# Attention stage of a two-layer decoder trunk: the same work per block in another order on each engine, norms cut in two, two buffers for queries and keys

## Chip, cores and metric

The kernel runs on all 8 cores of one Trainium2 chip, each core with its own share of the batch and no exchange between cores. The metric is the device time of the slowest core, in microseconds (us). In one execution of the kernel before, the median time was 3305.33 us over 3 runs (3304.32 to 3310.04).

## What is computed

One inference step of a two-layer decoder trunk. Layer 0 is a convolution module and a dense gated feed-forward network; from its output, keys and values are projected once. Layer 1 is what this document is about: sliding-window attention (16 query heads and 4 key heads of 64 channels, window 128, a learned sink per head, RMS-norm of every query and key head), then a top-2-of-8 expert network. Of the reference, cut to the part around attention:

```python
s = rms_norm(h, norm_kv); k = rms_norm((s @ w_k).reshape(..., 4, 64), k_norm); v = s @ w_v
q = rms_norm((rms_norm(h, norm_mix[1]) @ w_q).reshape(..., 4, 4, 64), q_norm)
s = einsum(q, k) * 64 ** -0.5            # query block n reads key blocks n-1 and n
e = exp(where(mask, s, -inf) - m); den = sum(e) + exp(sink - m)
h = h + (e / den @ v) @ w_o
hn = rms_norm(h, norm_ffn[1])            # goes to the router and to the experts
top_vals, top_idx = top_k(hn @ w_router + b_router, 2)
```

## The kernel before

A core has a prompt of 2048 rows, cut into 16 blocks of 128, and 16 sample rows as a seventeenth block (number 16, which goes first). The stages follow each other: convolution, dense feed-forward, its down projection with the gated embedding, attention with routing, experts, final stage. The attention stage is the loop at the end of `build`, 21 iterations i = 0 to 20, written out by hand as a software pipeline. Each engine executes its own instructions strictly in the order in which this loop issues them; semaphores are set by the scheduler class from what each instruction reads and writes.

In iteration i, block ord5[i] is projected, the block before it has its queries and keys turned, the block two before it has its scores, softmax and product with the values, the block three before it has its output projection, and its norm for the experts and its routing follow. The parts, in the order of iteration i before:

1. `x3_norm` (L1563): SyncE loads the residual rows of a block two iterations ahead, into one of 6 buffers.
2. `x3_turn` (L1579): TensorE turns the normed block (8 transposes into one PSUM bank), ScalarE copies it out (L939).
3. `x3_scale` (L1569) of the next block: ScalarE squares and sums (L944), VectorE adds epsilon (L948), GpSimd raises to the power -1/2 (L949), ScalarE scales (L1576).
4. `x_turn` (L1776): the normed output block of two iterations before is turned and copied, for the router.
5. `scores` (L1681) for group 0: TensorE, 4 matmuls into PSUM banks 0 and 1 (L1693); ScalarE takes the exponential (L1699); VectorE multiplies by the mask (L1701).
6. `kv_mm` (L1588): 8 matmuls of 512 columns (L1595); ScalarE copies keys into `qkf` and values into a bf16 buffer.
7. scores for group 1; `o_turn` (L1737): the attention output is turned, VectorE copies it (L941).
8. `q_mm` (L1608) half 0 (L1614, 8 matmuls), copied by ScalarE into `qkf`.
9. `pv` (L1704) group 0 (L1720, 8 matmuls into banks 4 to 6), scores group 2, `route_l` (L343).
10. `q_mm` half 1, `qk_norm` (L1619): ScalarE squares 1280 columns (L1623), VectorE sums over each head (L1624, L1625), GpSimd raises 20 columns to the power -1/2 (L1626).
11. pv 1, scores 3, `oproj` (L1744) half 0 (L1751, 8 matmuls; VectorE adds the result to the residual rows, L1756), pv 2, a waiting `wave_b`.
12. `qk_turn` (L1662) of the block before, oproj half 1, `o_norm` (L1760): SyncE stores the residual rows; ScalarE squares, VectorE adds epsilon, GpSimd takes the power, VectorE scales with the gain (L1770).
13. pv 3, `onorm` (L1724): VectorE, 3 sums, a reciprocal and 3 products (L1728, L1729, L1732), which release banks 4 to 6.
14. `qk_scale` (L1629): VectorE scales keys (L1633) and queries (L1654) by the power, GpSimd multiplies the keys by the gain, twice (L1656).

All transposes and projections share three PSUM banks in rotation (`mb`, L1558), so that a group of matmuls waits until the result three groups before it has been copied out. The scores always use banks 0 and 1, so a group of scores waits for the exponential of the group before. `qkf` is one buffer.

Iterations 2 to 6 have the work of the sample rows at their end (`s_scores`, `s_scores2`, `s_values`, and `s_load` of the next cached keys and values), iteration 6 also the output projection, norm and routing of block 16 in one sequence. When 5, 5, 4, 2 blocks (and block 16 alone) are routed, `wave_a` (L360) issues a part of their slot arithmetic, and `wave_b` (L382) an iteration later the rest: small VectorE operations to L424, then two indirect DMAs per block, issued by GpSimd (L161), which scatter the normed rows to the experts' areas, then further VectorE operations from L432 on, which wait until the scatters have read the slot numbers. After the loop the last wave goes out, the expert weights are requested, and the rows of expert 0 are loaded.

Of the kernel before, what the change touches and what calls it, by code (L numbers as in the profile page):

```python
# [24 lines left out]
EPS = 1e-6  # L25
# [813 lines left out]
def build():  # L839
# [647 lines left out]
    curW = Cursor(O_S5W, Arena.SIZE)  # L1487
    curL = Cursor(11264, O_S5W)
# [16 lines left out]
    qkf, qkf_r = t5([128, 1280], F32, 0)  # L1505
# [63 lines left out]
    def x3_scale(n_):  # L1569
# [5 lines left out]
        powh(ms, rs, ms_r, rs_r, n)  # L1575
# [12 lines left out]
    def kv_mm(n_, n, xT, xT_r):  # L1588

        b = mb()  # L1590

# [14 lines left out]
        return vb, vb_r  # L1606

    def q_mm(n_, n, xT, xT_r, h):  # L1608
# [10 lines left out]
    def qk_norm(n_, n, vb, vb_r):  # L1619
# [7 lines left out]
        return n_, n, vb, vb_r, rs, r_  # L1627

    def qk_scale(n_, n, vb, vb_r, rs, r_):  # L1629
# [130 lines left out]
    def o_norm(n_):  # L1760
# [8 lines left out]
        powh(ms, rs, ms_r, rs_r, n)  # L1769
# [98 lines left out]
    for k in range(2):  # L1868
        x3_norm(ord5[k])
    s_load(0)  # L1870
    xs_ = x3_scale(ord5[0])
    waves = {}
    qn = qt = on = xn_ = lt = wv = None
    pend_wave = None
    done_l = []
    for i in range(17 + 4):
        a = ord5[i] if i < 17 else None
        s_ = ord5[i - 2] if 3 <= i < 19 else None
        if i + 2 < 17:
            x3_norm(ord5[i + 2])  # L1880
        xt = x3_turn(*xs_) if xs_ is not None else None
        xs_ = x3_scale(ord5[i + 1]) if i + 1 < 17 else None
        lt = x_turn(*xn_) if xn_ is not None else None
        xn_ = None
        if s_ is not None:
            scores(s_, 0)
        if xt is not None:
            vb = kv_mm(*xt)
        if s_ is not None:
            scores(s_, 1)  # L1890
        ot = None
        if on is not None:
            ot = o_turn(*on)
            on = None
        if xt is not None:
            q_mm(*xt, 0)
# [3 lines left out]
        if lt is not None:  # L1900
            b = mb()
            tl.route_l(*lt, b, 0)
            done_l.append(lt[0])
            lt = None
        if xt is not None:
            q_mm(*xt, 1)
            qn = qk_norm(xt[0], xt[1], *vb)
        if s_ is not None:
            pv(s_, 1)
            scores(s_, 3)  # L1910
        if ot is not None:
            oproj(*ot, 0)
        if s_ is not None:
            pv(s_, 2)
        if pend_wave is not None:
# [136 lines left out]
```

How the kernel before makes its waits and increments, by code:

```python
    def wait(self, e, key, val):  # L87
        if val <= self.waited[e].get(key, 0):
            return
        self.E[e].wait_ge(self.semh[key], val)
        self.waited[e][key] = val
# [38 lines left out]
    def op(self, e, fn, r=(), w=(), part=False):  # L130
        xr = [x for x in r if x.excl]
        if xr:
            r = [x for x in r if not x.excl]
            w = list(w) + xr
        self.deps(e, r, w, part)
        inst = fn(self.E[e])
        self.cnt[e] += 1
        inst.then_inc(self.semh[e], 1)
        self.mark((e, self.cnt[e]), r, w, part)
# [1 line left out]
    def _land(self, inst, sem, r, w, part):  # L141
        self.cnt[sem] += 16
        inst.then_inc(self.semh[sem], 16)
        self.mark((sem, self.cnt[sem]), r, w, part)
```

## Time and profile before

| | us |
|---|---|
| median of 3 runs | 3305.33 |
| the profiled execution, its own time | 3307.96 |
| its span, slowest core (core 6) | 3306.6 |
| spans of all cores | 3280.7 to 3306.6 |
| attention loop, first key/query power to first expert matmul (L549) | 1255.3 to 1817.8 |

The profiled execution is 2.6 us over the median, and its time is 1.4 us over its span. Over the span TensorE is busy 75%, VectorE 31%, ScalarE 23%, GpSimd 18% of the time. In the page, PE is TensorE's matmuls, PEld its weight loads, DVE is VectorE, ACT ScalarE, POOL GpSimd, SP SyncE. A group of instructions is named by line and operation; "idle before" is the time for which its engine stood still just before it, with what ended that wait. On the page the experts' matmuls (L549 and L577) make up 36% of the chain that ended last, and "issue", time in which the chain's engine waited for nothing that the profile shows, 11%.

### The profile page before, as it was taken

Reading aid. Unit: us, or ns where it says so; the run is one execution under the profiler, and the core shown is the slowest. Engines: PE = TensorE matmul, PEld = TensorE weight load, DVE = VectorE, ACT = ScalarE, POOL = GpSimd, SP = SyncE. Lnnn points to the kernel's source line nnn. Section 1 sums busy time; section 2 is a strip of 40 time slices with the busy share of each in tenths; the row PEclk is TensorE's granted clock in tenths of the full one; section 3 lists DMA queues with packets and bytes.
Section 4 is the critical chain, followed back from the end, with each engine's and each line's share of the span. In section 5 each row is a group of like instructions: output and inputs, shape, how many; then the busy total and the mean of one; then the engine's idle time right before and its main releaser. Section 6 shows DMA issues by size and latency. Waiting matters only on the chain.

```text
span 3306.6 us, 43794 instructions; the slowest of 8 cores (3280.7 to 3306.6 us)
## 1 busy us (share of the span) xinstructions
PE 2479.0 (75%) x18881; PEld 1703.1 (52%) x18967; DVE 1032.2 (31%) x1532; ACT 745.1 (23%) x1074; POOL 583.1 (18%) x760
## 2 busy tenths in 40 slices
PE   5395323899989926654652999999999999997344
PEld 2253111455534413332321889988789888886111
DVE  3175455222223313444452212121112212121454
ACT  4111232111112124443430112111112111110111
POOL 1001221000000003323223111111112111110444
PEclk8597667899999966887775999999999999999677
DMA  7734311633032251101015999999889999981553
GB/s 178 130 78 101 96 64 58 170 58 71 1 89 72 78 155 52 52 33 64 32 55 119 177 166 187 180 173 188 135 146 175 184 165 185 146 143 46 131 132 100
DMA packets 156202, 377.38 MB, mean 114 GB/s; under 512 B 52296, under 2 KB 61512, under 8 KB 155008
## 3 DMA queue, kind: packets, MB, share of 16 engines
q0 software_dynamic: 69360, 230.65, 41.2%
q1 hardware_dynamic: 81360, 133.08, 13.6%
q10 hardware_dynamic: 5280, 10.75, 1.0%
q8 instruction: 151, 2.47, 0.3%
q14 instruction: 51, 0.42, 0.0%
HBM read 510.48 MB, written 74.24 MB: 177 GB/s over the span
## 4 chain that ended last, share of the span: by engine, by line
PE 60%; issue 11%; DVE 9%; POOL 8%; DMA 6%; ACT 5%; ACTq 1%; SPq 1%; DVEq 0%; POOLq 0%
PE pb L549 24%; PE pb L577 12%; PE pb L1361 9%; PE pb L1416 4%; PE pb L1087 3%; DMA arena<-sc 2%; DVE arena L941 2%; POOL arena L1626 1%; POOL arena L822 1%; PE pb L1614 1%; POOL arena L949 1%; PE pb L1289 1%; ACT arena L944 1%; ACT arena L1268 1%; POOL arena L161 1%
## 5 line engine op out<-in xcount | busy, mean ns | idle before, releaser
L549 PE MATMUL pb<-arena 128*128 128x0 bf16 x7168 | 795.6, 274 | 0.8 <-DVE arena L510 0.8
L549 PEld LDWEIGHTS pb<-arena 128*128 128x128 bf16 x7168 | 675.6, 98 | 117.6 <-issue 1.1
L577 PE MATMUL pb<-arena 128*128 128x0 bf16 x3584 | 404.9, 274 | 0.0
L557 DVE TENSOR_TENSOR arena<-arena,pb 128x640 bf16<-128x640 f32 x224 | 184.0, 822 | 654.3 <-PE pb L549 654.3
L577 PEld LDWEIGHTS pb<-arena 128*128 128x128 bf16 x3584 | 336.0, 98 | 56.5
L1361 PE MATMUL pb<-arena 128*128 128x413 bf16 (+1 forms) x1760 | 312.0, 341 | 11.8 <-ACT arena L1367 7.7
L556 ACT ACTIVATE arena<-pb 128x640 f32<-128x640 f32 x224 | 157.5, 703 | 622.2 <-PE pb L549 622.2
L930 PE MATMUL pb<-arena 128*128 128x128 bf16 (+1 forms) x1180 | 103.6, 244 | 255.8 <-DVE arena L1770 112.7
L1361 PEld LDWEIGHTS pb<-arena 128*128 128x128 bf16 x1760 | 172.8, 98 | 150.6 <-ACT arena L1367 8.1
L930 PEld LDWEIGHTS pb<-arena 128*128 128x128 bf16 (+1 forms) x1180 | 80.7, 111 | 285.6 <-DVE arena L1770 115.6
L149 POOL DMA_DIRECT2D arena<-moe_gu x224 | 118.3, 545 | 590.2 <-PE pb L549 254.2
L1289 PE MATMUL pb<-arena 128*128 128x512 bf16 (+1 forms) x264 | 77.6, 460 | 165.6 <-ACT arena L1268 165.6
L805 PE MATMUL pb<-arena 128*128 128x512 bf16 (+1 forms) x269 | 91.7, 513 | 135.2 <-DMA arena<-arena 134.6
L944 ACT ACTIVATE arena<-arena 128x1024 bf16<-128x1024 f32 (+1 forms) x85 | 89.8, 1056 | 421.0 <-DVE arena L1421 179.6
L1416 PE MATMUL pb<-arena 128*128 128x512 bf16 (+1 forms) x732 | 164.4, 381 | 1.9 <-DVE arena L1368 0.7
L949 POOL TENSOR_TENSOR arena<-arena 128x1 f32<-128x1 f32 (+1 forms) x102 | 56.0, 549 | 527.7 <-DVE arena L948 527.6
L1368 DVE TENSOR_TENSOR arena<-arena,pb 128x413 bf16<-128x413 f32 (+1 forms) x110 | 64.2, 585 | 256.2 <-PE pb L1361 235.2
L939 ACT COPY arena<-pb 128x1024 bf16<-128x1024 bf16 (+6 forms) x142 | 112.4, 793 | 114.0 <-PE pb L1614 47.2
L1289 PEld LDWEIGHTS pb<-arena 128*128 128x128 bf16 (+1 forms) x272 | 30.2, 115 | 207.0 <-ACT arena L1268 163.9
L149 POOL DMA_DIRECT2D arena<-moe_d x128 | 67.5, 528 | 386.7 <-PE pb L549 379.3
L805 PEld LDWEIGHTS pb<-arena 128*128 128x128 bf16 (+1 forms) x272 | 32.6, 125 | 194.6 <-DMA arena<-arena 142.9
L1087 PE MATMUL pb<-arena 128*128 128x413 bf16 (+1 forms) x640 | 126.9, 364 | 4.9 <-ACT arena L939 4.9
(198 smaller groups left out, 2433.2 us busy)
## 6 DMA issues: line engine op xcount, KB each, us to landing
arena<-moe_gu POOLq DMA_DIRECT2D x224, 512.0 KB, 32.6
arena<-moe_d POOLq DMA_DIRECT2D x128, 448.0 KB, 33.7
arena<-x SPq DMA_DIRECT2D x32, 512.0 KB, 5.4
arena<-ffn_gu POOLq DMA_DIRECT2D x22, 512.0 KB, 5.7
XG<-arena ACTq DMA_DIRECT2D x1, 10240.0 KB, 33.4
arena<-XG SPq DMA_DIRECT2D x8, 1280.0 KB, 40.3
YD<-arena SPq DMA_DIRECT2D x8, 1280.0 KB, 22.4
h1D<-arena SPq DMA_DIRECT2D x16, 512.0 KB, 3.0
```

The source lines that it names most:

```text
L149: inst = self.E[q].dma_start(out=out, in_=in_)
L549: last = e.matmul(bank(b + h, HALF).shape_from_register(sr), w[:, a, kc, :], xg[:, kc, h * HALF:(h + 1) * HALF].shape_from_register(sr), s ...
L556: S.op("act", lambda e: e.activation(out=sg, in_=self.two(bG), func=AF.Silu), r=[b_r[bG], b_r[bG + 1]], w=[sg_r])
L557: S.op("dve", lambda e: e.tensor_tensor(out=self.hx[:, f, :].rearrange("p (h c) -> p h c", h=2), in0=sg, in1=self.two(bU), op=ALU.mult), r ...
L577: last = e.matmul(bank(b + h, HALF).shape_from_register(sr), w[:, k, :], self.hx[:, f, h * HALF:(h + 1) * HALF].shape_from_register(sr), s ...
L805: last = e.matmul(bank(bG + h2, 512, n), xT[:, kc, 0:n], self.Wg[kc // 2][:, kc % 2, h2 * 512:(h2 + 1) * 512], start=(kc == 0), stop=(kc = ...
L930: last = e.transpose(out=bankb(bk)[:, k * 128:k * 128 + n], in_=src[0:n, (k0 + k) * 128:(k0 + k + 1) * 128], identity=identb[0:n, 0:n])
L944: S.op("act", lambda e: e.activation(out=junk, in_=src, func=AF.Square, scale=1.0 / 32.0, accum_out=ms), r=r, w=[w, jr])
L1087: last = e.matmul(bank(bk_, n), W[:, a, kc, :], xnT[:, kc, s0:s0 + n], start=(kc == 0), stop=(kc == 7))
L1289: last = e.matmul(bank(bk + h, 512, n), zT[:, kc, i * 128:i * 128 + n], W2[:, kc, h * 512:(h + 1) * 512], start=(kc == 0), stop=(kc == 7))
L1361: last = e.matmul(bank(bk_, n), W[:, a, kc, :], xnT2[:, kc, s0:s0 + n], start=(kc == 0), stop=(kc == 7))
L1416: last = e.matmul(bank(bk + h_, 512, n), lt, Wd[:, f, h_ * 512:(h_ + 1) * 512], start=(f == 0), stop=(f == NF - 1))
```

## The change

Nothing of the matrix work is removed or added. `x3_scale` and `o_norm` are each cut into a part that squares (`x3_sq`, `o_sq`) and a part that scales (`x3_scale`, `o_scale`); in both, the addition of epsilon moves from VectorE to GpSimd. `qk_scale` moves from the end of the iteration to near the beginning of the next; its two GpSimd products become a part of their own, `kk_gain`. `qkf` has two buffers. Block 16's norm and routing ride along in iteration 7. The load of residual rows goes to the end of the iteration. The stage's weights lie 4096 bytes higher, so that the second buffer has room.

```diff
-    curW = Cursor(O_S5W, Arena.SIZE)
-    curL = Cursor(11264, O_S5W)
+    curW = Cursor(O_S5W + 4096, Arena.SIZE)
+    curL = Cursor(11264, O_S5W + 4096)
...
-    qkf, qkf_r = t5([128, 1280], F32, 0)
+    qkb = t5([128, 1280], F32, 2)
...
+    def powp(ms, rs, ms_r, rs_r, n):
+        S.op("pool", lambda e: e.tensor_scalar(out=ms, in0=ms, scalar1=EPS, scalar2=None, op0=ALU.add), w=[ms_r])
+        S.op("pool", lambda e: e.tensor_tensor(out=rs, in0=ms, in1=nhalf[0:n, 0:1], op=ALU.pow), r=[ms_r, c_eps], w=[rs_r])
+
+    def x3_sq(n_):
...
         square(h[0:n, :], xh[0:n, :], ms, n, [h_r], ms_r, xh_r)
-        powh(ms, rs, ms_r, rs_r, n)
+        powp(ms, rs, ms_r, rs_r, n)
+        return n_, n, h, h_r, rs, rs_r, xh, xh_r
+
+    def x3_scale(n_, n, h, h_r, rs, rs_r, xh, xh_r):
         S.op("act", lambda e: e.activation(out=xh[0:n, :], in_=h[0:n, :], func=AF.Copy, scale=rs), r=[h_r, rs_r], w=[xh_r])
...
+        return n_, qh, qh_r, kk, kk_r, vb, vb_r, k4, qkf_r
+
+    def kk_gain(n_, qh, qh_r, kk, kk_r, vb, vb_r, k4, qkf_r):
+        if n_ < 16:
             for u_ in range(2):
                 S.op("pool", lambda e: e.tensor_tensor(out=kk[:, :, u_, :], in0=k4, in1=gqk.unsqueeze(1).to_broadcast([128, 4, 64]), op=ALU.mult),
```

The loop body after, in the order of issue (`s_` is the block whose attention is made):

```python
if s_ is not None: scores(s_, 0)
xt = x3_turn(*xs_)                       # turn of block ord5[i]
qt = qk_scale(*qn)                       # of the block before
scores(s_, 1)
rs_ = [o_sq(n_) for n_ in (rn, r16) if n_ is not None]
kk_gain(*qt)
vb = kv_mm(*xt)
rs_ = [o_scale(*v) for v in rs_]
pv(s_, 0); scores(s_, 2)
ot = o_turn(*on)
xq = x3_sq(ord5[i + 1])
q_mm(*xt, 0, *vb[2:4])
pv(s_, 1); scores(s_, 3)
lts = [x_turn(*v) for v in rs_]
xs_ = x3_scale(*xq)
q_mm(*xt, 1, *vb[2:4]); qn = qk_norm(xt[0], xt[1], *vb)
qk_turn(*qt[0:7])
pv(s_, 2); oproj(*ot, 0)
pv(s_, 3); on = onorm(s_)
oproj(*ot, 1); rn = ot[0]
tl.wave_b(...)                           # if one is waiting
for lt in lts: tl.route_l(*lt, mb(), 0)
...                                      # sample work, wave_a
x3_norm(ord5[i + 2])
```

## Rows read from the trace of the kernel before

**Rows 1.** Stretches: us, busy us (and instructions) by engine, granted TensorE clock, DMA share, GB/s

```profile
950.00:1158.00 208.00, 200.71 (x1008) 93.63 (x1030) 72.89 (x82) 44.19 (x56) 15.17 (x27) 1.00 0.23 74
1579.00:1606.00 27.00, 17.95 (x130) 9.00 (x132) 12.08 (x27) 12.97 (x18) 7.38 (x5) 0.75 0.11 40
```

**Rows 2.** Timeline of GpSimd: power of 20 columns, once per block (start, us, what)

```profile
1255.26 3.53 POOL L1626 TENSOR_TENSOR arena<-arena 16x20 f32<-16x20 f32 x1 [8.70 <-DVE arena L1625]
...
1383.31 3.91 POOL L1626 TENSOR_TENSOR arena<-arena 128x20 f32<-128x20 f32 x1 [13.09 <-DVE arena L1625]
...
1551.96 3.91 POOL L1626 TENSOR_TENSOR arena<-arena 128x20 f32<-128x20 f32 x1 [13.62 <-DVE arena L1625]
...
1578.93 3.91 POOL L1626 TENSOR_TENSOR arena<-arena 128x20 f32<-128x20 f32 x1 [13.95 <-DVE arena L1625]
...
1606.06 3.91 POOL L1626 TENSOR_TENSOR arena<-arena 128x20 f32<-128x20 f32 x1 [14.12 <-DVE arena L1625]
...
1661.34 3.91 POOL L1626 TENSOR_TENSOR arena<-arena 128x20 f32<-128x20 f32 x1 [12.07 <-DVE arena L1625]
...
1701.07 3.91 POOL L1626 TENSOR_TENSOR arena<-arena 128x20 f32<-128x20 f32 x1 [9.28 <-DVE arena L1625]
```

**Rows 3.** Groups by line and shape, 1552 to 1660 us: count, busy us, mean ns, idle before

```profile
L1699 ACT ACTIVATE arena<-pb 128x1024 bf16<-128x1024 f32 x16 | 16.3, 1020 | 0.1
L939 ACT COPY arena<-pb 128x1024 bf16<-128x1024 bf16 x12 | 12.0, 999 | 1.2 <-PE pb L930 1.2
L1701 DVE TENSOR_TENSOR arena<-arena 128x1024 bf16<-128x1024 bf16 x16 | 11.0, 690 | 33.8 <-ACT arena L1699 33.8
L1656 POOL TENSOR_TENSOR arena<-arena 128x256 bf16<-128x256 f32 x8 | 9.9, 1242 | 16.6 <-DVE arena L1633 16.3
L1624 DVE TENSOR_REDUCE arena<-arena 128x20 f32<-128x1280 f32 x4 | 5.9, 1486 | 6.6 <-ACT arena L1623 6.6
L1756 DVE TENSOR_TENSOR arena<-pb,arena 128x512 f32<-128x512 f32 x8 | 5.5, 688 | 6.9 <-PE pb L1751 6.9
L1770 DVE SCALAR_TENSOR_TENSOR arena<-arena 128x1024 bf16<-128x1024 f32 x4 | 5.1, 1284 | 2.9 <-POOL arena L949 2.9
L1623 ACT ACTIVATE arena<-arena 128x1280 f32<-128x1280 f32 x4 | 5.1, 1270 | 0.1
L1654 DVE TENSOR_TENSOR arena<-arena 128x1024 bf16<-128x1024 f32 x4 | 4.9, 1224 | 0.1
L949 POOL TENSOR_TENSOR arena<-arena 128x1 f32<-128x1 f32 x8 | 4.4, 547 | 8.6 <-DVE arena L948 8.6
```

**Rows 4.** Timeline inside one plain iteration

```profile
1586.24 1.03 PE L930 MATMUL pb<-arena 128*128 128x128 bf16 x8 [3.55 <-DVE arena L1770]
...
1591.97 1.15 ACT L1576 ACTIVATE arena<-arena 128x1024 bf16<-128x1024 f32 x1 [6.04 <-POOL arena L949]
...
1596.37 3.36 PE L1614 MATMUL pb<-arena 128*128 128x512 bf16 x8
...
1600.44 1.89 PE L1614 MATMUL pb<-arena 128*128 128x512 bf16 x7
...
1602.16 0.41 PE L1720 MATMUL pb<-arena 128*128 128x65 bf16 x8
```

**Rows 5.** Timeline of a wave of five blocks: VectorE's wait for ten scatters

```profile
1680.18 0.17 DVE L432 TENSOR_SCALAR arena<-arena 128x10 f32<-128x10 f32 x1 [14.55 <-DMA XG<-arena]
```

**Rows 6.** Timeline, iteration 16: GpSimd's product and a mask at once

```profile
1688.90 2.89 POOL L1656 TENSOR_TENSOR arena<-arena 128x256 bf16<-128x256 f32 x2 [4.08 <-DVE arena L1633]
...
1690.00 1.22 DVE L1701 TENSOR_TENSOR arena<-arena 128x1024 bf16<-128x1024 bf16 x1
```

**Rows 7.** Timeline after the last projection: squares of blocks 12 and 14; first expert's turns

```profile
1704.98 1.06 ACT L944 ACTIVATE arena<-arena 128x1024 bf16<-128x1024 f32 x1 [3.50 <-DVE arena L1756]
...
1739.65 1.06 ACT L944 ACTIVATE arena<-arena 128x1024 bf16<-128x1024 f32 x1 [4.43 <-DVE arena L1756]
...
1812.55 4.42 PE L502 MATMUL pb<-arena 128*128 128x128 bf16 x40 [35.20 <-issue]
```

More of the change, by code:

```diff
@@ L1590, in kv_mm @@
         b = mb()
+        qkf, qkf_r = qkb.next()
         def fk(e):
@@ L1867, in build @@
     S.dma("pool", Wo.rearrange("p k d -> p (k d)"), w_o, "wo", w=[Wo_r])
-    for k in range(2):
+    for k in range(3):
         x3_norm(ord5[k])
     s_load(0)
-    xs_ = x3_scale(ord5[0])
+    xs_ = x3_scale(*x3_sq(ord5[0]))
     waves = {}
-    qn = qt = on = xn_ = lt = wv = None
-    pend_wave = None
+    qn = qt = on = rn = pend_wave = None
+    r16 = None
     done_l = []
     for i in range(17 + 4):
-        a = ord5[i] if i < 17 else None
         s_ = ord5[i - 2] if 3 <= i < 19 else None
[L1879 to L1884, printed above, removed]
         if s_ is not None:
             scores(s_, 0)
+        xt = x3_turn(*xs_) if xs_ is not None else None
+        xs_ = None
+        qt = qk_scale(*qn) if qn is not None else None
+        qn = None
+        if s_ is not None:
+            scores(s_, 1)
+        rs_ = [o_sq(n_) for n_ in (rn, r16) if n_ is not None]
+        rn = r16 = None
+        if qt is not None:
+            kk_gain(*qt)
         if xt is not None:
             vb = kv_mm(*xt)
[L1889 to L1896, printed above, removed]
+        rs_ = [o_scale(*v) for v in rs_]
         if s_ is not None:
@@ L1899, in build @@
             scores(s_, 2)
-        if lt is not None:
+        ot = o_turn(*on) if on is not None else None
+        on = None
+        xq = x3_sq(ord5[i + 1]) if i + 1 < 17 else None
+        if xt is not None:
+            q_mm(*xt, 0, *vb[2:4])
+        if s_ is not None:
+            pv(s_, 1)
+            scores(s_, 3)
+        lts = [x_turn(*v) for v in rs_]
+        if xq is not None:
+            xs_ = x3_scale(*xq)
+        if xt is not None:
+            q_mm(*xt, 1, *vb[2:4])
+            qn = qk_norm(xt[0], xt[1], *vb)
+        if qt is not None:
+            qk_turn(*qt[0:7])
+        if s_ is not None:
+            pv(s_, 2)
+        if ot is not None:
+            oproj(*ot, 0)
+        if s_ is not None:
+            pv(s_, 3)
+            on = onorm(s_)
+        if ot is not None:
+            oproj(*ot, 1)
+            rn = ot[0]
+        if pend_wave is not None:
+            tl.wave_b(*pend_wave, mb(), 0, xns)
+            pend_wave = None
+        for lt in lts:
             b = mb()
@@ L1903, in build @@
             done_l.append(lt[0])
[L1904 to L1915, printed above, removed]
-            tl.wave_b(*pend_wave, mb(), 0, xns)
-            pend_wave = None
-        if qt is not None:
-            qk_turn(*qt)
-            qt = None
-        if ot is not None:
-            oproj(*ot, 1)
-            xn_ = o_norm(ot[0])
-        if s_ is not None:
-            pv(s_, 3)
-            on = onorm(s_)
-        if qn is not None:
-            qt = qk_scale(*qn)
-            qn = None
         if i == 2:
@@ L1941, in build @@
                 oproj(16, OT16, OT16_r, half)
[L1942 to L1947 removed]
+            r16 = 16
+        for b0, b1 in ((0, 5), (5, 10), (10, 14), (14, 16), (16, 17)):
+            if b1 - 1 in done_l and b1 not in waves and pend_wave is None:
                 waves[b1] = 1
[L1949 removed]
                 pend_wave = tl.wave_a(b0, b1)
+        if 1 <= i and i + 2 < 17:
+            x3_norm(ord5[i + 2])
+    assert len(waves) == 5
     tl.wave_b(*pend_wave, mb(), 0, xns)
```

24 lines of the change are left out of this document (9 added, 15 removed).

## Prediction

> **What bounds the kernel now.** I read the spans first: all cores lie within 0.8%, so one core's trace is enough. Then the chain that ended last: the experts' matmuls dominate it, but the change doesn't touch them. The stage that it does touch shows as "issue" and one GpSimd line, time in which nobody is busy. So I read that stage by stretches. In the stage before, TensorE is busy for 200.71 of 208 us at a granted clock of 1.00; in a plain iteration of attention it is busy for 17.95 of 27, ScalarE 12.97, VectorE 12.08, GpSimd 7.38, at a clock of 0.75 [rows 1]. No engine is the bound; the period is. The GpSimd power of 20 columns comes once per block, and two of its starts, 1578.93 and 1606.06, give a period of 27.1 us [rows 2].
>
> The timeline shows what fills it: one loop through all engines. From the end of q's second half: copy, square of 1280 columns 1.27, sum over heads 1.49, mask 0.69, addition 0.69, the second output projection 1.9, addition 0.69, square 1.06, GpSimd's power 0.55, scaling with the gain 1.28, `onorm` and the key scaling (about 2.7), GpSimd's two key products 2.48, its power for the next block 0.55 [rows 3]. Only then can ScalarE scale the next block; it has idled 6.04 us for that [rows 4]. Scale 1.15, copy 1.0, exponential 1.02, then TensorE's second scores, a turn, and q's first half, which takes 3.36 us at the low clock (1.2 GHz) [rows 3, 4]; then q's second half, and round again. The products for the keys of one block stand between the power of the next block and its scaling only because they were issued there. All of this is order, not need.
>
> **The change, part by part.** I walk one new iteration, time 0 at the first scores, each engine in its issue order, each step at the later of its engine being free and its input ready. Terms [rows 3, 4]: exponential 1.0, ScalarE copy of a block 0.9 until the next instruction and 1.05 until a reader, square 1.05, scale 1.05, head square 1.2, mask and addition 0.65, gain 1.2, head sum 1.5, 8 matmuls of 512 columns 1.72 to the next group at the high clock (1600.44 to 1602.16), half-size ScalarE copies 0.4 to 0.55.
>
> ScalarE: exponential 0 at 0.45, x copy 1.4, exponential 1 at 2.25, o square 3.2, k and v copies 4.35, exponential 2 at 5.2, x square 6.1, q copy 7.45, exponential 3 at 8.0, router copy 8.9, x scale 9.8, q copy 10.85, head square 11.4, q turned copy 12.6.
> TensorE: scores 0 and turn at 0, scores 1 at 1.5, kv 2.4, scores 2 at 4.6, o turn 5.0, q half at 5.5, scores 3 at 7.6, router turn 7.9, q half 8.4, turns 10.1, output projection 11.5 (waits for the PSUM bank of the q copy), second one 13.6 (bank of the turned q), router 15.3, next iteration 15.6.
> VectorE: mask 0 at 3.1, keys and queries scaled to 5.3, mask 1, gain 5.9, mask 2 at 7.1, o copy, mask 3 at 9.05, head sum 12.7, key copy, addition 14.65, `onorm` 15.25, addition 17.5, router to 18.7, which is 3.1 of the next iteration.
>
> Two limits meet: TensorE's own work with short waits, 15.6 us; and the loop from kv (2.4) over q, head square, head sum, `onorm` and the second addition (done at 18.1) to the next kv, which takes over its PSUM bank, 15.7 us. The critical loop of before is cut at three places: x's scaling waits for a square made 3.7 us earlier; the key products stand ahead of x's power but have 4 us of room; o's square and gain are spread over the next iteration.
>
> The moves one by one. **Epsilon on GpSimd**: two additions more per block, not in the trace on that engine; at least nothing beyond what VectorE's hand-over took, at most a power each, 0.55 [rows 3]. I take 0.5, since the nearest row is a GpSimd operation of the same shape. GpSimd then has 7.4 + 1.0 us of 15.7, and the walk has both in it. On VectorE it frees 0.3. **`qk_scale` at the start**: behind it stand mask 1, the gain, and TensorE's pv. Its power starts at 14.4 and ends at 18.3, that is 2.6 of the next iteration, before VectorE is there (3.7): covered by `onorm`; without that cover up to 3.9 per block. **Two `qkf`**: keep the new k copy (4.35) from waiting for the key products of the old block, which end at 8.0; nothing by themselves. **Loads at the end** of the iteration: SyncE's queue holds store, sample loads, load; the load has almost an iteration until its square: nothing. If that cover fails, a landing of some 3 us. **Weights 4096 bytes higher**: same queue, same predecessors' end: nothing.
>
> To 15.7 I add what the walk leaves out: moments at the low clock, where a group costs up to 3.36 instead of 1.89 [rows 4], and the meeting of GpSimd and VectorE. In a late iteration a mask beside the key products took 1.22 instead of 0.69, and those 2.89 instead of 2.48 [rows 6, 3]; now two VectorE operations per block lie beside them. Together I take 1.8: **period 17.5**, bounds 15.7 and 20.5 (next paragraph).
>
> The Trainium skill ("SBUF — State Buffer", section "Who interferes with whom") says that VectorE instructions with two SBUF inputs and GpSimd exclude each other for a whole instruction. The row agrees only in part: queries are scaled in 1.22 us, two SBUF inputs, right beside the products [rows 3], undisturbed. By the page the rival below would hold; by the rows 1 us at most.
>
> Sums over the stage, intervals between the powers [rows 2]:
> - Iterations 0 to 6, 128.05 us, the pipeline filling and sample work: two of 11, four of 20.5, 21, 23, 23 (17.5 or less, plus a sample chain of some 6 that before lay in idle time): 109.5. Gain 18.5.
> - 6 to 11, 168.65 us: block 16's projection 5.5 on top (its norm and turn no longer stall everyone), its wave 7, a routing iteration 1, and a wave of five. There VectorE waits 14.55 us for ten scatters on GpSimd [rows 5]; about 3 of it plus small operations stay beside TensorE's work, and 14.5 remain. 5 x 17.5 + 28 = 115.5. Gain 53.
> - 11 to 15, 109.4 us: 4 x 17.5 + 1 = 71. Gain 38.4.
> - 15 to 16, 39.7 us, the second wave: 32. Gain 7.7.
> - The tail [rows 7]: 34.7 us between the squares of blocks 12 and 14, without projections: 24. From block 14's square to the first expert 72.9 us, mostly scatters and the load of rows: 5.5 less. Gain 16.
>
> Together 134 us: 3308.0 - 134 = 3174 for the profiled execution, and, as the median lies 2.6 under it, 3172. A microsecond of period is worth 14 us.
>
> **The rivals.**
> *Exclusion of VectorE and GpSimd* (the page above as a mechanism here). GpSimd's 8.4 us per block all push VectorE's 12 away: a period of 20.5. For it: rows 6. Against: the undisturbed scaling. 3308 - 134 + 42 = 3216, median 3214. Chance 0.12.
> *A new wait*: waves and sample work take all that the shorter period gives around them, say since powers now stand behind scatters in GpSimd's queue; only the plain intervals gain: 38.4 + 7 of ten in 6 to 11 at about 20 + 11 in the tail, some 70: 3236. Against: during a scatter VectorE stands anyway. Chance 0.08.
> *Slower*: TensorE stays at 1.2 GHz. Place: every group of the iteration. A group of 512 columns then takes 3.4 instead of 1.72 [rows 4], five of them 17.1; with turns, scores and pv at the same ratio 26.2, and with waits for the first exponential and copy 27.5. Sample work, until now in idle time, adds to it: 3308 + 14 x 0.4 + 20 = about 3334. It decides once TensorE's work plus waits exceeds 27.1 us, so nearly always low. Against: in the stage before, 96% busy, the clock is 1.00 [rows 1]; in the old loop a turn takes 1.03 us, half speed, right after TensorE has stood for 3.55 us [rows 4], and the walk has no stand over 1.1 us. Chance 0.04.
> *It doesn't do what it says*: another edge, a bank or buffer, keeps the loop at 27: 3300 to 3308. Against: I followed all eleven bank hand-overs in the walk. Chance 0.03.
>
> **How the numbers follow.** The forecast, 3172, has 0.73. Its bounds are 3172 - 25 = 3147 at a period of 15.7 and, at 19, 3193; 5 us off at the lower end for a sample part that hides better. With the first rival, 3214, and its own spread, the range 3142 to 3222 holds 0.84. A measurement of this kernel can tell about 0.2% (7 us) from no change. Faster by more: 0.73 + 0.12 + 0.08 and a little of the last, 0.94; within it 0.02; slower 0.04.
>
> **What would show it.** Right: 16 intervals between the first and the last GpSimd power adding up to about 328 instead of 446 us, plain ones 16 to 19; TensorE's clock over 0.9 there and idle under 3 us an iteration; ScalarE's scale without the 6 us ahead of it; VectorE's waits in the waves as long as before; stages before and behind unchanged. The period is wrong if masks or key products get longer (first rival), or if VectorE waits for the 20-column power at L1633's place. The forecast falls with a clock under 0.8 in plain iterations or a period over 22.

## Result and profile after

The change makes the kernel faster: the ratio of its time to that of the kernel before is 0.9643, with a 95% interval of 0.9608 to 0.9679, which is 118 us less. Two runs of the first measurement and two of a later one (3198.2, 3171.6, 3183.5, 3180.3 us) have a mean of 3183; the forecast was 3172, the range 3142 to 3222. Some executions of either kernel have the cores of one die at a lower clock; they are left out of all comparisons here, and where too few others remained, no ratio is given but the single times. In the profiled execution after (3198.2 us, slowest core 2) the matmuls of the dense feed-forward, which the change doesn't touch, took 361 ns each on cores 0 to 3 against 341 before, 339.7 us busy on core 2 against 312.0; on core 4 they took 341 ns and 312.3 us. The attention stage behind it is of the same length on both groups of cores. From the pages of the kernel before and after:

```profile
L1361 PE MATMUL pb<-arena 128*128 128x413 bf16 (+1 forms) x1760 | 312.0, 341 | 11.8 <-ACT arena L1367 7.7
...
L1361 PE MATMUL pb<-arena 128*128 128x413 bf16 (+1 forms) x1760 | 339.7, 361 | 11.6 <-ACT arena L1367 7.5
```

Stretches of the kernel after (us, busy us and instructions by engine, granted clock, DMA share, GB/s), the stage ahead of attention, one plain iteration and one interval with a wave of five blocks:

```profile
980.00:1190.00 210.00, 202.30 (x1017) 94.28 (x1035) 74.11 (x85) 44.59 (x56) 15.16 (x27) 1.00 0.22 73
1552.60:1569.30 16.70, 13.81 (x132) 7.80 (x133) 12.62 (x25) 13.00 (x17) 8.78 (x8) 1.00 0.19 64
1482.80:1519.30 36.50, 17.54 (x141) 9.21 (x143) 16.77 (x49) 12.99 (x17) 18.87 (x18) 0.67 0.25 101
```

Against [rows 1], ScalarE has the same 13.0 us of work and VectorE 12.6 instead of 12.1, but in 16.7 us and not 27. TensorE's work itself shrank from 17.95 to 13.81: the same matmuls at a clock of 1.00 instead of 0.75. That holds for plain iterations; with a wave of five the clock is 0.67. GpSimd's 20-column powers, as in [rows 2]:

```profile
1285.46 3.53 POOL L1635 TENSOR_TENSOR arena<-arena 16x20 f32<-16x20 f32 x1 [5.36 <-DVE arena L1634]
...
1390.91 3.54 POOL L1635 TENSOR_TENSOR arena<-arena 128x20 f32<-128x20 f32 x1 [6.58 <-DVE arena L1634]
...
1519.27 3.54 POOL L1635 TENSOR_TENSOR arena<-arena 128x20 f32<-128x20 f32 x1 [6.72 <-DVE arena L1634]
...
1535.94 3.54 POOL L1635 TENSOR_TENSOR arena<-arena 128x20 f32<-128x20 f32 x1 [5.56 <-DVE arena L1634]
...
1590.06 3.54 POOL L1635 TENSOR_TENSOR arena<-arena 128x20 f32<-128x20 f32 x1 [6.29 <-DVE arena L1634]
...
1626.84 3.54 POOL L1635 TENSOR_TENSOR arena<-arena 128x20 f32<-128x20 f32 x1 [9.15 <-DVE arena L1634]
```

The plain interval is 1535.94 - 1519.27 = 16.67 us, and the next two are the same. The sixteen intervals together are 341.4 us instead of 445.8. The groups of three plain iterations after, 1519.3 to 1569.3 us, as [rows 3]:

```profile
L1712 ACT ACTIVATE arena<-pb 128x1024 bf16<-128x1024 f32 x12 | 12.4, 1030 | 7.5 <-PE pb L1706 7.5
L1714 DVE TENSOR_TENSOR arena<-arena 128x1024 bf16<-128x1024 bf16 x12 | 9.7, 811 | 0.0
L1669 POOL TENSOR_TENSOR arena<-arena 128x256 bf16<-128x256 f32 x6 | 6.9, 1155 | 0.2
L1786 DVE SCALAR_TENSOR_TENSOR arena<-arena 128x1024 bf16<-128x1024 f32 x3 | 5.2, 1742 | 1.4 <-POOL arena L1572 1.4
L1571 POOL TENSOR_SCALAR arena<-arena 128x1 f32<-128x1 f32 x6 | 4.5, 750 | 6.3 <-ACT arena L944 6.1
L1633 DVE TENSOR_REDUCE arena<-arena 128x20 f32<-128x1280 f32 x3 | 4.5, 1485 | 9.9 <-ACT arena L1632 9.9
L1623 PEld LDWEIGHTS pb<-arena 128*128 128x128 bf16 x48 | 4.3, 98 | 8.1 <-DVE arena L941 3.9
L1572 POOL TENSOR_TENSOR arena<-arena 128x1 f32<-128x1 f32 x6 | 4.3, 715 | 0.5
L1584 ACT ACTIVATE arena<-arena 128x1024 bf16<-128x1024 f32 x3 | 3.4, 1149 | 0.0
```

ScalarE's scale (L1584, before L1576) no longer stands 6 us idle ahead of GpSimd. Masks wait for nothing. The gain (L1786, before L1770) has grown from 1.28 to 1.74 us, masks from 0.69 to 0.81 on average. The timeline of one such iteration shows where:

```profile
1558.17 0.95 POOL L1571 TENSOR_SCALAR arena<-arena 128x1 f32<-128x1 f32 x1 [2.03 <-ACT arena L944]
...
1560.04 2.39 POOL L1669 TENSOR_TENSOR arena<-arena 128x256 bf16<-128x256 f32 x2
1560.11 1.74 DVE L1786 SCALAR_TENSOR_TENSOR arena<-arena 128x1024 bf16<-128x1024 f32 x1 [0.46 <-POOL arena L1572]
...
1561.77 1.21 DVE L1714 TENSOR_TENSOR arena<-arena 128x1024 bf16<-128x1024 bf16 x1
...
1562.91 0.68 DVE L941 COPY arena<-pb 128x1024 bf16<-128x1024 bf16 x1
...
1563.87 1.67 PE L1623 MATMUL pb<-arena 128*128 128x512 bf16 x7 [1.34 <-ACT arena L939]
```

Gain and third mask lie beside the key products and take 0.46 and 0.52 us longer; then the turned output is copied (L941), and q's second half, which takes over its PSUM bank, has TensorE stand for 1.3 us. The row of the matmuls names ScalarE's copy (L939), which ends 0.15 us after L941; the group's weight loads wait for L941, 3.9 us in three iterations. Read on, the chain goes over head square, head sum, additions, division, scaling and masks to the next gain, as the loop that now sets 16.67 us. The three changes of order below put this to the test.

By segment, forecast against the two profiles:

| segment | before | forecast after | after |
|---|---|---|---|
| iterations 0 to 6 | 128.1 | 109.5 | 105.5 |
| 6 to 11 (block 16's wave, one of five) | 168.7 | 115.5 | 128.4 |
| 11 to 15 (three plain) | 109.4 | 71 | 70.8 |
| 15 to 16 (wave of five) | 39.7 | 32 | 36.8 |
| last power to the first expert's turns | 111.5 | 95.5 | 87.1 |
| sum | 557.3 | 423.5 | 428.4 |

The end of the last row is, in the timeline after (as in [rows 7]):

```profile
1713.89 2.40 PE L502 MATMUL pb<-arena 128*128 128x128 bf16 x21 [19.90 <-issue]
```

### The profile page after: what moved, and what is told of

It is laid out like the page before. It is cut to its first block, busy times and chain, and to the rows that moved or that the text cites. A ratio compares the mean times of both kernels' runs of the same rounds, so it can differ in the third digit from the quotient of the medians.

```text
span 3196.9 us, 43778 instructions; the slowest of 8 cores (3160.2 to 3196.9 us)
## 1 busy us (share of the span) xinstructions
PE 2486.7 (78%) x18881; PEld 1712.3 (54%) x18967; DVE 1031.8 (32%) x1498; ACT 742.5 (23%) x1074; POOL 599.1 (19%) x794
## 4 chain that ended last, share of the span: by engine, by line
PE 64%; DVE 10%; issue 7%; DMA 6%; POOL 6%; ACT 5%; ACTq 1%; SPq 1%; DVEq 0%; POOLq 0%
PE pb L549 25%; PE pb L577 12%; PE pb L1361 10%; PE pb L1416 5%; PE pb L1087 3%; DVE arena L941 2%; DMA arena<-sc 2%; POOL arena L822 2%; PE pb L1289 1%; PE pb L1623 1%; ACT arena L939 1%; ACT arena L944 1%; ACT arena L1268 1%; POOL arena L161 1%; PE pb L930 1%
## 5 line engine op out<-in xcount | busy, mean ns | idle before, releaser
L549 PEld LDWEIGHTS pb<-arena 128*128 128x128 bf16 x7168 | 679.0, 98 | 113.6 <-issue 1.1
L577 PEld LDWEIGHTS pb<-arena 128*128 128x128 bf16 x3584 | 337.6, 98 | 54.5
L1361 PE MATMUL pb<-arena 128*128 128x413 bf16 (+1 forms) x1760 | 339.7, 361 | 11.6 <-ACT arena L1367 7.5
L1361 PEld LDWEIGHTS pb<-arena 128*128 128x128 bf16 x1760 | 181.4, 103 | 169.6 <-ACT arena L1367 7.9
L930 PE MATMUL pb<-arena 128*128 128x128 bf16 (+1 forms) x1180 | 96.1, 234 | 169.6 <-ACT arena L1584 60.4
L939 ACT COPY arena<-pb 128x1024 bf16<-128x1024 bf16 (+6 forms) x142 | 112.5, 793 | 101.9 <-PE pb L930 42.9
L1087 PE MATMUL pb<-arena 128*128 128x413 bf16 (+1 forms) x640 | 126.0, 362 | 4.9 <-ACT arena L939 4.9
L1367 ACT ACTIVATE arena<-pb 128x413 f32<-128x413 f32 (+1 forms) x110 | 56.6, 516 | 296.5 <-PE pb L1361 269.8
## 6 DMA issues: line engine op xcount, KB each, us to landing
XG<-arena ACTq DMA_DIRECT2D x1, 10240.0 KB, 36.4
```

Of the source, the lines that this page charges most:

```text
L549: last = e.matmul(bank(b + h, HALF).shape_from_register(sr), w[:, a, kc, :], xg[:, kc, h * HALF:(h + 1) * HALF].shape_from_register(sr), s ...
L577: last = e.matmul(bank(b + h, HALF).shape_from_register(sr), w[:, k, :], self.hx[:, f, h * HALF:(h + 1) * HALF].shape_from_register(sr), s ...
L930: last = e.transpose(out=bankb(bk)[:, k * 128:k * 128 + n], in_=src[0:n, (k0 + k) * 128:(k0 + k + 1) * 128], identity=identb[0:n, 0:n])
L939: S.op("act", lambda e: e.copy(out=dst, in_=src), r=r, w=w, part=part)
L1087: last = e.matmul(bank(bk_, n), W[:, a, kc, :], xnT[:, kc, s0:s0 + n], start=(kc == 0), stop=(kc == 7))
L1361: last = e.matmul(bank(bk_, n), W[:, a, kc, :], xnT2[:, kc, s0:s0 + n], start=(kc == 0), stop=(kc == 7))
```

## Experiments

The three plain intervals and the sum of all sixteen are read in each kernel's own profile, on all eight cores. Single values below are those of core 1 unless said otherwise; the means, with the range over the cores, are (us):

| kernel | plain intervals | sum of sixteen |
|---|---|---|
| before | 27.0 to 27.2 | 444.3 (442.7 to 446.3) |
| changed, measured again | 16.7 | 341.1 (338.9 to 343.4) |
| one buffer | 19.6 to 20.3 | 368.9 (367.9 to 370.2) |
| epsilon on VectorE | 17.1 | 345.7 (344.4 to 346.3) |
| before, one cut alone | 24.2 to 25.6 | 431.3 (428.1 to 434.0) |
| late exponential | 16.7 | 329.4 (328.5 to 331.2) |
| no wait for the scatters | 16.7 | 326.3 (324.9 to 327.5) |
| both, scatters handed out | 18.7 to 20.5, then 16.7 twice | 301.0 (299.4 to 302.8) |
| turned output early | 16.2 | 335.8 (334.9 to 337.5) |
| key products behind | 15.8 | 336.8 (335.0 to 338.1) |
| scaling at the end | 16.7 | 356.4 (354.9 to 357.9) |
| all that helped | 17.2 to 18.7, then 15.8 twice | 287.7 (284.5 to 290.2) |

### The changed kernel again

No edit.

> The changed kernel again, unaltered, beside the kernel before. Its first profile shows plain intervals of 16.67 us and, on the cores whose dense feed-forward ran at full clock, spans of 3160 to 3171 us. Theory 'the whole gain lies between the first key/query power and the first expert matmul, about 129 us': ratio to the kernel before 0.960 to 0.961. Rival 'the 0.9643 of the first runs is the true value, some stage outside attention gives back 13 us': ratio 0.964 and a stage outside attention that is longer on all cores.

Measured: plain intervals of 16.7 us on every core; 3180.3 and 3183.5 us beside eight runs of the kernel before with 3300.7 to 3311.1 (mean 3305.7): ratios of 0.962 and 0.963. On core 1, 428.3 us pass from its first power to its first expert matmul, against 561.0 on the same core in the profile before, and 1479.6 us from there to its end, against 1477.6. So the stage gains 126 to 133 us by core (mean 130). In the mean over the cores, what lies ahead of it takes 1252.0 us against 1249.9 before and what lies behind it 1480.6 against 1479.6, while single cores differ by up to 17 us in either: nothing outside gives back more than some 3 us. The time of the kernel is that of the slowest of eight cores, which takes some us of the gain; the expected ratio of 0.960 was too low, the rival's longer stage isn't there.

### One buffer for queries and keys

```diff
-    qkb = t5([128, 1280], F32, 2)
+    qkb = t5([128, 1280], F32, 1)
+    t5([128, 1280], F32, 0)
```

> The changed kernel with one buffer for queries and keys instead of two (its second one left as unused room, so that every other address stays). Theory 'the second buffer is a condition of the new order': the copy of the new keys, at 5.8 us after the start of the iteration's 20-column power, must wait for GpSimd's key products, which end at 9.8: ScalarE stands 4 us in every block, plain interval about 20.5, time 14 x 3.8 = 53 us over the changed kernel. Rival 'other waits on ScalarE take it in': plain interval under 17.5, under 12 us.

Measured: plain intervals 19.6 to 20.3 us, times 3194.7 and 3204.6. The waits of core 1, 1497 to 1557 us (who waited for whom, us in total, times, longest):

```profile
ACT arena L939 <- POOL arena L1670: 13.1, 3, 4.4
```

The wait is the one named, 4.4 us a block, and the period grows by 2.9 to 3.6. The sum grew by 28 us, not the 53 expected of the time: where a wave or the sample work already holds the iteration, the wait hides in it (37.1 instead of 36.3 with five blocks). The second buffer carries some 3.3 us of the plain period. That it gains nothing by itself was forecast; no run has it alone in the kernel before.

### Epsilon back on VectorE

```diff
-        S.op("pool", lambda e: e.tensor_scalar(out=ms, in0=ms, scalar1=EPS, scalar2=None, op0=ALU.add), w=[ms_r])
+        S.op("dve", lambda e: e.tensor_scalar(out=ms, in0=ms, scalar1=EPS, scalar2=None, op0=ALU.add), w=[ms_r])
```

> The changed kernel with the addition of epsilon of both norms back on VectorE. Theory 'in its issue order VectorE reaches it late': for the output norm behind the second mask, for the input norm behind the copy of the turned output; the gain starts 0.3 us later, ScalarE's scale 0.5; plain interval 17.0 to 17.2, 4 to 7 us over the changed kernel. Rival 'GpSimd's two additions (0.95 and 0.55 us) and their meeting with VectorE cost more than that': plain interval 16.0 to 16.6, 2 to 9 us under it.

Measured: plain interval 17.1 on every core, mean sum 345.7 against 341.1. The expected size, 0.4 us an iteration. The time doesn't resolve it: 3174.2 to 3178.7 us in four runs and 3188.8 and 3208.8 in two, ratio 0.9618 (0.9597 to 0.9638), not apart from the changed kernel. The move of epsilon is worth some 5 us in the stage and none that can be measured in the whole.

### One cut alone, in the kernel before

```diff
-        if i + 2 < 17:
-            x3_norm(ord5[i + 2])
...
         if s_ is not None:
             scores(s_, 1)
+        xn_ = o_norm(rn) if rn is not None else None
+        rn = None
+        if i + 2 < 17:
+            x3_norm(ord5[i + 2])
...
+        lt = x_turn(*xn_) if xn_ is not None else None
...
-            xn_ = o_norm(ot[0])
+            rn = ot[0]
```

A first form of it left the load of residual rows at the start of the iteration, so that a block's rows were overwritten before their output norm: it computed that norm and the routing of other rows.

> The kernel before with one of the cuts alone: the output norm of a block (square, epsilon, power, gain) is made in the next iteration, behind the second scores, and its turn behind the third; all else as before. Theory 'one loop fills the period': the output norm stood in it between the second addition and the division of the attention output, 3.25 us; plain interval 27.1 - 3.2 = 23.9, 14 x 3.2 = 45 us under the kernel before. Rival 'another loop of the same length stands behind it': plain interval 26 or more, under 15 us.

That form had plain intervals of 24.3 to 25.6 us and one time of 3311.0 us. Its intervals are those of the next form, but as it computes something else, the next one is the one to go by. The form of the diff:

> The kernel before with one of the cuts alone: the output norm of a block (square, epsilon, power, gain) is made in the next iteration, behind the second scores, and its turn behind the third; the load of residual rows is issued right behind it; all else as before. Theory 'one loop fills the period': the output norm stood in it between the second addition and the division of the attention output, 3.25 us; plain interval 27.1 - 3.2 = 23.9, 14 x 3.2 = 45 us under the kernel before. Rival 'another loop of the same length stands behind it': plain interval 26 or more, under 15 us.

Measured on core 1:

```profile
1536.65 3.91 POOL L1626 TENSOR_TENSOR arena<-arena 128x20 f32<-128x20 f32 x1 [10.02 <-DVE arena L1625]
...
1561.17 3.91 POOL L1626 TENSOR_TENSOR arena<-arena 128x20 f32<-128x20 f32 x1 [9.37 <-DVE arena L1625]
...
1585.48 3.91 POOL L1626 TENSOR_TENSOR arena<-arena 128x20 f32<-128x20 f32 x1 [9.03 <-DVE arena L1625]
```

24.5 and 24.3 us against 27.1, but the third plain interval is 25.6. On all cores the mean is 24.8: one link of 3.25 us taken out shortens the loop by 2.3, by 2.8 at best. The stretches show what else moves, TensorE's clock (core 1, columns as in [rows 1]):

```profile
1561.17:1585.48 24.31, 15.54 (x132) 8.21 (x132) 12.29 (x27) 13.09 (x18) 7.44 (x5) 0.93 0.13 44
1585.48:1611.10 25.62, 16.84 (x132) 8.70 (x132) 12.32 (x27) 13.13 (x18) 7.47 (x6) 0.87 0.11 42
```

The instructions are the same, but q's first half, which lies on the loop, took 2.76 us in the one and 3.62 in the other:

```profile
1574.30 2.76 PE L1614 MATMUL pb<-arena 128*128 128x512 bf16 x8
...
1598.61 3.62 PE L1614 MATMUL pb<-arena 128*128 128x512 bf16 x8
```

So the link was part of the loop, and the rival (26 or more) is out; but the length of the loop also depends on the clock that TensorE has on it, and part of the gain of a cut is clock won back, in this run and in the change itself. The times, 3281.7 and 3291.3, are only 15 to 25 us under the kernel before, not 45: the other intervals gained less (the sum 13 us in the mean). One cut gives about a quarter of the plain gain of 10.4 us.

### The small exponential of the routing

```diff
-        S.op("act", lambda e: e.activation(out=t1, in_=t1, func=AF.Exp), w=[s_r])
...
         W = k * 8
+        S.op("act", lambda e: e.activation(out=t1, in_=t1, func=AF.Exp), w=[s_r])
```

> The changed kernel; ScalarE's small exponential for the routing moves from the end of an iteration (where it waits for VectorE's slot arithmetic, with the next iteration's first score exponential behind it) to the start of the wave an iteration later. Theory 'this wait is why the intervals with a first routing half are 20.8 to 22 us and not 16.7': they fall to about 17.5, and the time by 4 x 4 = 16 us. Rival 'VectorE's ten small operations alone make them long': they stay over 19.5, under 6 us.

The line is moved from the end of `wave_a` to the start of `wave_b`. The reason to try it stands in the timeline of the changed kernel:

```profile
1574.67 0.21 ACT L379 ACTIVATE arena<-arena 128x5 f32<-128x5 f32 x1 [6.31 <-DVE arena L378]
1574.79 1.00 ACT L1712 ACTIVATE arena<-pb 128x1024 bf16<-128x1024 f32 x1
```

ScalarE stands 6.31 us before an operation on five columns, and the next block's first exponential stands behind it. Measured: the three intervals after a first routing half go from 22.1, 21.9 and 20.8 to 19.0, 17.3 and 17.3, the mean sum from 341.1 to 329.4; ratio 0.9585 (0.9551 to 0.9620). The theory holds, though one of the three stays at 18.3 to 19.0 by core, over the expected 17.5. There are three such intervals among the sixteen, so 12 us there, not 16; the times can't tell the two apart.

### No wait of VectorE for the scatters

```diff
-        g_r = self.g_r[b0]
+        g_r, f_r = Res(), Res()
         for b in range(b0, b1):
-            self.g_r[b] = g_r
+            self.g_r[b] = f_r
...
-        dv(lambda e: e.tensor_scalar(out=oq, in0=q, scalar1=1.0, scalar2=None, op0=ALU.min), r=[s_r], w=[g_r])
+        dv(lambda e: e.tensor_scalar(out=oq, in0=q, scalar1=1.0, scalar2=None, op0=ALU.min), r=[s_r], w=[f_r])
```

and likewise for the other results behind it, which no scatter reads.

> The changed kernel; the slot numbers that the scatters read and the results that VectorE writes after them are tracked apart, so that VectorE no longer waits for the scatters (14.4 us with ten of them). Theory 'GpSimd's queue is the next wait': ten scatters hold GpSimd 12.7 us all the same, the power of the output norm stands behind them, and VectorE stops at the gain instead; an interval with five blocks goes from 36.4 to about 31, 20 us in all. Rival 'VectorE's wait was the cost': such an interval falls to 22 or less, 40 us or more in all.

Measured: the intervals with five blocks go from 36.4 to 31.5, block 16's from 25.5 to 20.3, the mean sum from 341.1 to 326.3, 15 us of the 20 expected; times 3157.6 and 3162.7. The timeline of core 1 names the next wait:

```profile
1474.14 1.75 DVE L1786 SCALAR_TENSOR_TENSOR arena<-arena 128x1024 bf16<-128x1024 f32 x1 [8.59 <-POOL arena L1571]
```

VectorE now stops 8.59 us at the gain, whose power stands behind the scatters on GpSimd. Theory confirmed in kind, and in size for the interval with five blocks (31 expected).

### Both, and the scatters handed out

```diff
+            tl.wave_b(*pend_wave, mb(), 0, xns, 2 if i < 17 else 99)
...
+        for _ in range(2):
+            if tl.todo:
+                f_, b_ = tl.todo.pop(0)
+                f_(b_)
```

`wave_b` issues the scatters of two blocks and leaves the others in `todo`, from which each iteration takes two blocks behind `onorm`.

> The changed kernel with both of the edits (exponential at the start of the wave, no wait of VectorE) and the scatters handed out over iterations, those of two blocks at a time (5 us of GpSimd, which is busy 8.8 of 16.7 us in a plain iteration). Theory 'wait and queue were the cost of the waves': intervals with or after a wave 18 to 22 us, 2 x 14 + 16 + 5 = about 50 us under the changed kernel, ratio to the kernel before 0.948. Rival 'scatters and the other work meet on GpSimd or in the transfers': each of the three intervals after a wave is longer by 4 us or more, under 30 us in all.

Measured: ratio 0.9478 (0.9455 to 0.9501), five runs of 3131.9 to 3138.9 us. The sum is 301.3; the intervals with five blocks are 23.5 and 22.5, the one after the first 18.7 (20.3 to 20.5 on four other cores), then 16.7. GpSimd on core 1, spread out:

```profile
1461.11 3.54 POOL L1642 TENSOR_TENSOR arena<-arena 128x20 f32<-128x20 f32 x1 [6.57 <-DVE arena L1641]
1464.83 1.08 POOL L161 DMA_INDIRECT XG<-arena  x1 [0.18 <-issue]
...
1470.56 2.38 POOL L1676 TENSOR_TENSOR arena<-arena 128x256 bf16<-128x256 f32 x2
```

So of the 19.7 us by which a five-block interval lay over a plain one, 5 went with VectorE's wait and 8 to 9 more with GpSimd's queue, of which 2 to 4 us return in the interval after the first. Some 6 us are left in such an interval; VectorE's small operations and the four scatters before the gain are there still, and no run takes them apart. The ratio is the expected one; the five-block intervals lie somewhat over the expected 18 to 22 us, and the interval after the first is 2.0 to 3.8 us longer than a plain one, under the rival's 4, the next two not at all.

### What sets 16.67 us: three changes of order

Turned output copied ahead of the gain:

```diff
+        ot = o_turn(*on) if on is not None else None
+        on = None
         rs_ = [o_scale(*v) for v in rs_]
         if s_ is not None:
             pv(s_, 0)
             scores(s_, 2)
-        ot = o_turn(*on) if on is not None else None
-        on = None
```

> The changed kernel; the turn of the attention output is issued ahead of the gain and of the first product with the values, so that VectorE copies it out before it makes the gain. Theory 'the 16.7 us are the loop head sum, additions, division, key and query scaling, masks, gain, copy of the turned output, q's second half (which waits 1.3 us for that copy's bank), head square': q's second half no longer waits, plain interval 15.7 to 16.1, 14 x 0.8 = 11 us under the changed kernel. Rival 'ScalarE, busy 13.0 of 16.7 us, bounds it with its waits': plain interval stays within 0.2 of 16.7.

Measured: plain interval 16.2, mean sum 5.3 us lower, ratio 0.9614 (0.9586 to 0.9641), not apart from the changed kernel's. Half a microsecond a period, less than expected (15.7 to 16.1) but beyond the rival's bound: the bank hand-over is a link of the loop.

Key products behind the next block's power:

```diff
-        if qt is not None:
-            kk_gain(*qt)
         if xt is not None:
             vb = kv_mm(*xt)
...
         xq = x3_sq(ord5[i + 1]) if i + 1 < 17 else None
+        if qt is not None:
+            kk_gain(*qt)
```

> The changed kernel; GpSimd's two key products are issued behind the square and power for the next block, so that they no longer lie beside the gain and the third mask. Theory 'VectorE and GpSimd slow each other and this is on the path': the gain goes from 1.74 to 1.3 us, the third mask from 1.21 to 0.7, plain interval 15.7 to 16.2, about 10 us less. Rival 'the meeting only moves to the next instructions or costs nothing on the path': plain interval within 0.2 of 16.7.

Measured: plain interval 15.8 on every core, mean sum 4.3 us lower; times 3172.2 and 3174.2. The groups of core 1, 1500 to 1545 us:

```profile
L1714 DVE TENSOR_TENSOR arena<-arena 128x1024 bf16<-128x1024 bf16 x10 | 7.2, 716 | 0.8 <-ACT arena L1712 0.8
...
L1669 POOL TENSOR_TENSOR arena<-arena 128x256 bf16<-128x256 f32 x6 | 5.3, 889 | 0.2
...
L1786 DVE SCALAR_TENSOR_TENSOR arena<-arena 128x1024 bf16<-128x1024 f32 x3 | 3.9, 1285 | 1.4 <-POOL arena L1572 1.4
```

The gain is back at 1.285 us, masks at 0.72, and the key products take 0.89 us each instead of 1.16, still with one mask beside them. TensorE's wait for the bank of the turned output falls from 1.34 to 0.34 us. The meeting of the two engines was worth 0.9 us of every plain period; the other intervals gained less, so the sum fell by 4 us and not the 10 expected of the time.

Scaling of keys and queries back at the end of the iteration:

```diff
-        qt = qk_scale(*qn) if qn is not None else None
-        qn = None
+        qt, qe = qe, None
...
             done_l.append(lt[0])
+        if qn is not None:
+            qe = qk_scale(*qn)
+            qn = None
```

> The changed kernel; the scaling of keys and queries goes back to the end of the iteration (behind the router's operations), the key products stay where they are. Theory 'its place is worth something because VectorE then makes the first mask before it': the mask comes 1.6 us later, with it the first product with the values, the third scores and what ScalarE makes of them; plain interval 17.2 to 17.8, 7 to 15 us more. Rival 'the place is indifferent, VectorE makes the same work': within 0.2 of 16.7.

Measured: plain interval 16.7, unchanged: in a plain iteration the rival is right, since both places lie on the same chain of VectorE. But the mean sum is 356.4, 15 us more, and the ratio 0.9687 (0.9659 to 0.9715): on core 1 23.2 instead of 19.8 in the first iteration with scores, 38.8 instead of 36.3 with five blocks. The place earns its time where VectorE has been held up.

### All edits that helped

The last: spread scatters, late exponential, no wait, turned output early, key products behind.

> The changed kernel with all edits that helped: exponential at the start of the wave, no wait of VectorE for the scatters, scatters handed out over iterations, the turned output copied ahead of the gain, key products behind the next block's power. Theory 'the gains of waves and plain intervals add up': plain intervals 15.2 to 15.8, the 16 intervals 290 to 297 us instead of 301, time 5 to 10 us under the kernel with spread scatters, ratio to the kernel before 0.945 to 0.947. Rival 'another limit, TensorE's and ScalarE's own order, takes it': 300 us or more, ratio 0.948 as before.

Measured: ratio 0.9435 (0.9408 to 0.9462), 3118.2 to 3123.1 us; plain intervals 15.8, but for the one behind the first wave of five, mean sum 287.7. That is 186 us under the kernel before and some 60 under the changed one. The sum came out a little lower than the expected 290: against the spread scatters alone, the intervals with five blocks fell from 22.4 to 23.7 us to 20.9 to 22.9, and those with a first routing half from 17.3 to 16.3.

## Why the prediction was right, point by point

- **One loop, no engine, fills the period**: right. In a plain iteration TensorE's clock went to 1.00 and its idle time to 2.9 us, ScalarE's 6 us ahead of the scale are gone. The single cut, with 2.3 of 3.25 us, shows that its link lay on the loop. What the prediction counts as order alone is partly clock: q's first half, a link of the loop, took 3.36 us before [rows 4] and 1.89 after. No run separates the two: with the single cut, too, the clock rose, from 0.75 to 0.93.
- **Period 17.5, bounds 15.7 and 20.5**: measured 16.67. The walk gave 15.7, and 1.0 of the 1.8 us laid on top was due: the meeting of VectorE and GpSimd, for which 1 us at most was allowed, is worth 0.9 (the key products moved behind the power); without it 15.8 is measured, beside the walk's 15.7. The 0.8 for moments at the low clock was not needed. One sign named for the first rival came all the same: gain and masks got longer, and the period did not leave its bounds by it.
- **The lock as the Trainium skill has it** ("SBUF — State Buffer", "Who interferes with whom"): the row [rows 6] held, the exclusion for a whole instruction that the page states didn't. Gain and products run at once, 1560.11 to 1561.85 beside 1560.04 to 1562.43; the gain is a third longer than without them, the products are half as long again (2.39 us for two against 1.53). What I read wrongly in [rows 3]: only VectorE's side was undisturbed there. The products take 1.24 us each there, beside the query scaling, and 0.77 where no VectorE instruction lies beside them (key products behind the power, core 1):

```profile
1484.61 1.53 POOL L1669 TENSOR_TENSOR arena<-arena 128x256 bf16<-128x256 f32 x2
```

GpSimd was the one that paid.
- **Epsilon on GpSimd**: taken at 0.5 us; in a plain iteration the two additions take 0.95 and 0.55 us, mean 0.75, by their neighbours on VectorE, and the new place is still 0.4 us an iteration better than the old one.
- **Two buffers, `qk_scale` early**: the buffers were said to gain nothing by themselves. The second one is a condition: in the walk the key products end 3.65 us after the copy of the new keys (8.0 against 4.35), and with one buffer waits of up to 4.4 came. Whether the early scaling serves the plain iteration was left open by the walk; it doesn't, it serves the waves and the first iteration with scores, 15 us in the sum.
- **Waves**: the step that was mis-sized. I had 14.5 us left of a wave of five and 1 us for a first routing half; 19.7 and 4.1 to 5.4 were measured. In the first I counted VectorE's wait of 14.55 but hid 3 us of it and the small operations beside TensorE's work. The timeline after shows that nothing hides, since the first mask stands behind the wait, and behind the mask stand TensorE and ScalarE:

```profile
1504.29 0.17 DVE L432 TENSOR_SCALAR arena<-arena 128x10 f32<-128x10 f32 x1 [14.62 <-DMA XG<-arena]
...
1507.18 0.62 PE L1733 MATMUL pb<-arena 128*128 128x65 bf16 x8 [15.31 <-DVE arena L1714]
...
1508.38 1.02 ACT L1712 ACTIVATE arena<-pb 128x1024 bf16<-128x1024 f32 x1 [15.69 <-PE pb L1706]
```

The wait of 14.6 and VectorE's small operations on either side of it, 3.3 and 1.6 us, add up to 19.5. In the second I missed that ScalarE waits for VectorE there. In the segments 6 to 11 and 15 to 16, two first halves are 8.0 us longer than forecast, the two waves of five 9.3, block 16's wave 1.0, its projection 0.7 shorter: the 17.6 us by which these segments came out over the forecast.
- **Tail**: 24.4 us gained, 16 forecast, and not where it was put. Between the squares of blocks 12 and 14 the gain is 5.2 us (34.7 to 29.5, forecast 24), from block 14's square to the first expert's turns 19.4 (72.9 to 53.5, forecast 5.5 less). Why was not looked into.
- **The stage's sum**: 428.4 against 423.5, but by errors that cancel: by segment -4.0, +12.9, -0.2, +4.8 and -8.4 us. That it came within 5 us is luck; the same holds for the third segment, where the shorter period hides a routing half of 4.1 us instead of 1.
- **The whole**: 118 us measured against 134. The stage accounts for 129 in the profiles; the rest is put down to the slowest core of eight, whose distance from the others changes from run to run (the spans of the later run lie 27 us apart, 3154.9 to 3182.2). The two profiled executions themselves differ by 109.7 us, since the feed-forward took 27.7 us more in the second.

Of the rivals, exclusion did not come: the two engines slow each other and still overlap, which costs 0.9 of the 4.8 us by which that rival's period of 20.5 lies over the walk. The new wait behind the scatters exists, as the second in a row of two, and 8 to 9 us of a five-block interval go with it once the first is gone. The clock did not stay low in plain iterations, where it was 1.00, but it did fall elsewhere: over all sixteen intervals it is 0.84 (0.76 before), with a wave of five 0.67, where TensorE had stood for 15.31 us and 7 of the 8 matmuls of q's first half behind it took 2.57 us; in a plain iteration 7 of q's matmuls took 1.67. The sign "over 0.9" holds for the plain ones alone.

## What to carry to other kernels

When no engine is busy for more than two thirds of a period, write down the loop link by link with its durations and walk a proposed order with each engine's queue before changing anything; each link taken out shortens the loop by at most its own length, and only until the next chain takes over. Look at TensorE's granted clock in every version: links on TensorE get shorter or longer with it. A gain per iteration counts only in iterations that nothing else holds, so multiply it by their number and not by all. A tiny operation at the end of an engine's queue (five columns on ScalarE, the record-keeping behind a scatter on VectorE) can hold a whole iteration behind it: look for those first, they are cheap to move.

## Not expected of the hardware

- GpSimd's two products of 256 columns take 1.53 us together with nothing beside them on VectorE, 1.85 beside one mask, 2.39 beside gain and mask, 2.56 beside the query scaling, 2.89 beside scaling and mask, all VectorE instructions that read two operands from SBUF. Of those, the gain (f32 in) takes 1.74 instead of 1.28 and the mask (bf16) 1.21 instead of 0.68, while the query scaling takes 1.22 with the products beside it and without. The 20-column power took 3.91 us in the kernel before, where masks ran beside it, and 3.54 after, where none did, as in its first three blocks before.
- GpSimd's addition on a single column takes 0.23 us with VectorE idle (behind the scatters, 1502.54 us; also the median over the kernel after), 0.55 beside a mask (1562.52 us) and 0.95 beside the query scaling (1558.17 us).
- With TensorE's idle gaps of 3.5 us gone, it took 4 us less for its own work in a plain iteration, 17.95 to 13.81: the granted clock was 1.00, its higher level (2.4 GHz), where it had been 0.75.
